# Attention with the values as the stationary operand, a position-major bias table, and ScalarE taking over the rounding and the head outputs

## The reference

```
s_win = einsum(q, k_band) + bias        # window of 8 x 16 positions, relative position bias
s_win = where(col_ok, s_win, NEG_INF)
s_ctx = einsum(q, k_ctx)
p = softmax(concat([s_win, s_ctx]))
o = p_win @ v_band + p_ctx @ v_ctx      # 8 heads of 64 columns
y = real(fft2(f))                       # Fourier branch, 4 groups of 128 channels
mix = (sigmoid(ga) * (y @ w_fourier) + sigmoid(gb) * (o @ w_na_out)) @ w_out
```

## Time and profile before

| | |
|---|---|
| median of 3 runs | 2649.9 us (2649.89 to 2650.17) |
| the profiled execution | 2653.5 us |
| its span | 2651.7 us |
| PE busy | 2619.6 us, 99% |
| PE weight loads busy | 2589.6 us, 98% |
| DVE busy | 2066.4 us, 78% |
| ACT busy | 1059.4 us, 40% |
| mean DMA rate | 111 GB/s |

### The profile page before, as it was taken

The page is one execution under the profiler, slowest core; times in us unless marked ns, Lnnn a source line. Parts: engine busy times, 40 slices in busy tenths (PEclk is TensorE's granted clock), DMA queues, the critical chain, the costliest instruction groups (busy, mean ns, idle before and its releaser), DMA issues.

```text
span 2651.7 us, 46222 instructions
## 1 busy us (share of the span) xinstructions
PE 2619.6 (99%) x18014; PEld 2589.6 (98%) x18014; DVE 2066.4 (78%) x3929; ACT 1059.4 (40%) x1866; POOL 0.2 (0%) x4
## 2 busy tenths in 40 slices
PE   8999999999999999999999999999999999999998
PEld 8999999999999999999999999999999999999997
DVE  7787986867766888798688888777786568987877
ACT  5145253533222534525352534534332225253453
POOL 0000000000000000000000000000000000000000
PEclk9999999999999999999999999999999999999998
DMA  7433422312333132242223242222313322324321
GB/s 281 138 111 106 166 93 98 120 69 98 112 127 124 67 112 96 93 161 95 96 96 120 87 150 104 95 106 98 114 65 127 137 69 101 115 87 151 113 100 58
DMA packets 77804, 295.38 MB, mean 111 GB/s; under 512 B 25168, under 2 KB 31568, under 8 KB 54096
## 3 DMA queue, kind: packets, MB, share of 16 engines
q1 hardware_dynamic: 51552, 211.16, 22.4%
q10 hardware_dynamic: 26096, 82.16, 8.8%
HBM read 289.62 MB, written 6.82 MB: 112 GB/s over the span
## 4 chain that ended last, share of the span: by engine, by line
PE 93%; DVE 4%; DMA 1%; issue 1%; ACT 1%; SPq 0%; ACTq 0%; DVEq 0%
PE psum L799 10%; PE psum L804 10%; PE psum L803 10%; PE psum L539 5%; PE psum L542 5%; PE psum L541 5%; PE psum L588 4%; PE psum L587 4%; PE psum L584 4%; PE psum L1102 3%; PE psum L1105 3%; PE psum L1104 3%; PE psum L688 2%; PE psum L693 2%; PE psum L692 2%; PE psum L900 2%
## 5 line engine op out<-in xcount | busy, mean ns | idle before, releaser
L804 PE MATMUL psum<-Th,w_lo 128*128 128x320 f32 x1024 | 316.4, 309 | 0.0
L799 PE MATMUL psum<-Th,w_hi 128*128 128x320 f32 x1024 | 316.3, 309 | 0.0
L803 PE MATMUL psum<-Tl,w_hi 128*128 128x320 f32 x1024 | 316.1, 309 | 0.0
L1163 ACT ACTIVATE w_hi<-w_raw 128x2048 fp32r<-128x2048 f32 x96 | 183.5, 1911 | 273.4 <-DVE acc L1728 119.8
L539 PE MATMUL psum<-Hh,w_hi 128*128 128x320 f32 x896 | 277.2, 309 | 3.3 <-DVE Hl L2032 2.4
L542 PE MATMUL psum<-Hh,w_lo 128*128 128x320 f32 x896 | 276.7, 309 | 0.0
L541 PE MATMUL psum<-Hl,w_hi 128*128 128x320 f32 x896 | 276.6, 309 | 0.0
L1645 DVE TENSOR_TENSOR w_lo<-w_raw,w_hi 128x2048 fp32r<-128x2048 f32 x96 | 219.6, 2288 | 54.5 <-ACT w_hi L1163 53.5
L799 PE MATMUL psum<-Uh,w_hi 128*128 128x320 f32 x768 | 237.5, 309 | 0.0
L803 PE MATMUL psum<-Ul,w_hi 128*128 128x320 f32 x768 | 237.2, 309 | 0.0
L804 PE MATMUL psum<-Uh,w_lo 128*128 128x320 f32 x768 | 236.6, 308 | 0.0
(11 more groups left out here) (348 smaller groups left out, 7243.8 us busy)
## 6 DMA issues: line engine op xcount, KB each, us to landing
w_raw<-in_wstream SPq DMA_DIRECT2D x184, 1024.0 KB, 4.8
ada_w<-in_ada ACTq DMA_DIRECT2D x145, 512.0 KB, 3.4
first_w<-in_ada SPq DMA_DIRECT2D x9, 512.0 KB, 14.8
first_w<-in_ada_first SPq DMA_DIRECT2D x6, 512.0 KB, 8.8
gath<-in_rpb SPq DMA_DIRECT2D x128, 24.0 KB, 3.5
G<-gath ACTq DMA_DIRECT2D x4, 768.0 KB, 4.7
X<-in_xT SPq DMA_DIRECT2D x8, 320.0 KB, 15.3
yT<-X SPq DMA_DIRECT2D x8, 192.0 KB, 1.9
```

What stands on the lines that cost most here:

```text
L799: m1 = pe.matmul(out, hi[:, k, :], rh, start=(start and k == 0), stop=False, skip_group_check=not start)
L803: pe.matmul(out, hi[:, k, :], rl, start=False, stop=False, skip_group_check=not start)
L804: mm = pe.matmul(out, lo[:, k, :], rh, start=False, stop=(k == 3), skip_group_check=not start)
L1163: act.activation(hi, w_raw[:, r, :, :], ACT.Copy).then_inc(s_whi, 1)
```

## The change

1. The values become the stationary operand, the turned probabilities move. The outputs of the two heads of a step go to the partitions 0 to 63 and 64 to 127 of one PSUM bank, tile by tile in turn. The output is then already turned: `Otok` becomes `OT`, the 20 transposes go, and one pair of VectorE instructions splits all of it.
2. The scale by the reciprocal sum can't be applied to such an output (it would differ by column), so VectorE scales the probabilities in place, before they are turned, at the start of step n for pair n-1. The transposes wait for that (`probs_scaled`) and no longer for the exponentials.
3. ScalarE stores the head outputs (one 128x128 copy per step) and rounds the Fourier pieces; VectorE keeps the subtraction.
4. The bias table is stored with the grid row innermost, so that L2269's operand is contiguous; it is gathered with 16 DMAs in place of 128. The tables are made at steps 1, 2, 3, 4 and (two) 6, not 1, 2, 3, 5, 6, 7.
5. The second `round_tile` of a stage moves on ScalarE from step 6 to step 5, and the second `low_tile` on VectorE from step 7 to step 5.

More of the change, by code:

```diff
@@ L469, in _ @@
         def _(pe):
-            C = make("tile use full h u mean sum sqsum var att sc max exp pt ptc o of fill fev mix mrg opsplit prod snap tlow".split(), u=0)
+            C = make("tile use full h u mean sum sqsum var att sc max scl pt ptc o of fill fev mix mrg opsplit prod snap tlow".split(), u=0)
             tile, use = C["tile"], C["use"]
@@ L890, in attention @@
                     if n >= 2:
[L891 to L903, removed]
+                        pe.wait_ge(s_ptc, C["ptc"].next(2))
+                        if n == 2:
+                            all_evacuated()
+                        if n >= 4:
+                            pe.wait_ge(s_of, C["of"].next())
+                        j = UNIT[2 * n - 4][1]
[7 more added lines that the diff above has]
+                        mm.then_inc(s_o, 1)
+                        C["o"].next()
                     if 1 <= n <= STEPS:
@@ L1143, in _ @@
         def _(act):
-            C = make("use full func mods u32 u xc sq added var std xn y att max exp pt ptc o mrg ada kv wraw whi wsum prod snap late add hsum tsum".split())
+            C = make("use full func mods u32 u xc sq added var std xn y att max exp pt ptc o of fill fhi mrg ada kv wraw whi wsum prod snap late add hsum tsum".split())
             use = C["use"]
@@ L1499, in ffn, with attention @@
                     last_products(l, s, [spare_f, spare_g], True, LATE_PAIRS)
-            def attention():
-                for n in range(STEPS + 1):
+            def attention(hh):
+                for n in range(STEPS + 2):
+                    if 1 <= n <= PIECES:
+                        round_piece(n - 1)
                     if n < STEPS:
@@ L1623, in _ @@
         def _(dve):
-            C = make("use full func h mods u32 u mean sum sq sqsum added std xc xn att kv max sc exp of fill fev pt o mix mrg ada dve whi ophi opsplit wsum prod snap late add hsum hhi tsum thi tlow".split())
+            C = make("use full func h mods u32 u mean sum sq sqsum added std xc xn att kv max sc exp scl of fhi fill fev pt o mix mrg ada dve whi ophi opsplit wsum prod snap late add hsum hhi tsum thi tlow".split())
             use = C["use"]
@@ L2273, in attention @@
-                    if n >= 2:
[L2274 to L2280, removed]
-                    if n in (2, 7):
+                    if n == 1:
+                        dve.wait_ge(s_att, C["att"].next(64 if hh == 0 else 32))
@@ new lines, in attention @@
+                    if n in BIAS_STEPS:
+                        dve.wait_ge(s_max, C["max"].at())
+                    for step in BIAS_STEPS.get(n, ()):
+                        p, kind = divmod(step, 3)
+                        for h in (2 * p, 2 * p + 1):
+                            g = G[:, h, BIAS_OFF[kind] * ROWS:(BIAS_OFF[kind] + WCOLS) * ROWS]
+                            slot = 2 * (step % 2) + h % 2
+                            dve.tensor_tensor(bm[:, slot, 0:256], mask[:, kind, :], g, ALU.subtract).then_inc(s_dve, 1)
+                            bias_at[step] = C["dve"].next()
@@ L2394, in mixing @@
                     dve.wait_ge(s_kv, C["kv"].next(32))
-                for c in range(4):
-                    u = use_no[0]
-                    dve.wait_ge(s_full, C["full"].next())
-                    split_from(bank(u, 0, 0, LAT), Oh[:, c, 0:LAT], Ol[:, c, 0:LAT])
-                    free(split_from(bank(u, 1, 0, P), Oh[:, c, LAT:T], Ol[:, c, LAT:T]))
+                dve.wait_ge(s_of, C["of"].at())
+                split_from(OT[:, :, :], Oh[:, :, :], Ol[:, :, :])
                 link(dve.tensor_copy(Yh[:, :, :], y32[:, :, :]))
@@ L2524, in window_masks, with bias_rows @@
     return out.reshape(P, 3, WCOLS * ROWS)
+def bias_rows(rpb):
+    wide = np.pad(rpb.reshape(DEPTH * HEADS, 2 * ROWS - 1, 2 * WIN - 1), ((0, 0), (0, 0), (16, 17)))
+    rows = [wide[:, ROWS - 1 - r:2 * ROWS - 1 - r].transpose(0, 2, 1) for r in range(ROWS)]
+    return np.ascontiguousarray(np.stack(rows, axis=1)).reshape(DEPTH * HEADS, ROWS, -1)
 def small_waves():
```

89 lines of the change are left out of this document (39 added, 50 removed).

## The result

| | before | changed |
|---|---|---|
| median | 2650.0 us (2649.9 to 2651.0, 4 runs) | 2633.8 us (2633.2 to 2634.6, 4 runs) |
| profiled execution | 2653.5 | 2633.2 |
| its span | 2651.7 | 2631.4 |
| PE busy | 2619.6 | 2594.3 |
| DVE busy | 2066.4 | 2046.9 |

The ratio is 0.9933, with a 95% interval of 0.9922 to 0.9944: 16.3 us faster between the medians, where 14 were forecast.

The account below looks back on a forecast made before the run. TensorE, busy 99%, bounds the kernel. Stages gain 10.4 us and layer ends 3.6, together 14.0: the profiled 2653.5 becomes 2639.5, and 3.6 less for the median gives 2636 us (chance 0.50), range 2626 to 2649.

Parts of the forecast that it names:

- step 6: Attention stage: TensorE's transposes wait 1.8 us for VectorE's scaling queued behind `low_tile`; the step 1.3 us longer.
- step 3: Attention stage: transposes wait for the first scaling behind VectorE's weight subtraction, a gap of 0.7 us.
- Head outputs: TensorE's 12 instructions of a latent step fall from 1.39 to 0.76 us; context steps from 0.50 to 0.32.
- step 4: Attention stage, a latent step without new waits: the plain gain of the head outputs, 0.63 us.
- not side by side: Rival: the two heads don't run in parallel on TensorE, heads stay at 1.4 us; 2648 us, chance 0.15.
- exposed weight loads: Rival: head outputs' weight loads can't hide beside matmuls, 2.9 us a step in place of 0.76; 2700 us, chance 0.10.
- Step 1: First stage of a layer: scaling ends the transposes 0.8 us late, two times in the program.
- Step 5: Attention stage: piece 5 waits for VectorE's subtraction of piece 4, so the gain is 0.48 us.
- Steps 7 to 11: End of an attention stage, 17.0 us before: shorter heads and no `low_tile` wait in step 8, gain 3.5 us.
- A scaled row: VectorE's `tensor_scalar` of 384 elements: 0.36 us for one, 0.65 for two in a row.
- End of a layer: Last heads to gates: 2.82 us becomes 1.0, gain 1.8, twice: 3.6 us.
- Clock: TensorE's clock falls twice, in the first layer's stages, 1.5 us each; rival of six or more falls 2642 us, chance 0.15.

Follow-up runs that it names:

- run 1: Changed kernel with the three tiles of one head issued before those of the other, not alternating; 2638.5 us.
- run 2: Changed kernel without VectorE's scaling of the probabilities, transposes waiting for the exponentials, head outputs left undivided; 2625.4 us.
- run 3: Changed kernel with the second rounding and subtraction of a weight tile back in steps 6 and 7; 2633.3 us.
- run 6: Changed kernel with VectorE's weight tiles at the ends of steps 3 and 6, not 2 and 5, and one bias table each at 5 and 6; 2626.6 us.
- run 7: Changed kernel with ScalarE's two DMA issues for the context keys and values behind its first exponentials, not ahead; 2632.1 us.
- run 8: Changed kernel with the moves of run 6 and run 7 together; 2625.4 us.

## Why the prediction was right

The measured 2633.8 lies 2.2 us below the forecast of 2636, and the forecast's case was the one that came. That the total is so near is in part luck: of the terms of the last stage, step 6 came 0.45 us shorter than forecast and step 3 0.37, while the gains of the other steps together were 0.4 smaller. TensorE's busy time fell by 25.3 us and the span by 20.3, so the new waits are 5 us more than the old ones. By its steps:

- **Head outputs**: 0.76 us forecast, 0.81 measured (0.108 for each of six pairs and 0.16 once). The six transposes behind them take 0.05 longer than before (0.63 and 0.58), which the forecast left out: a latent step without waits, step 4, is 0.53 us shorter, not 0.63. Context steps: 0.32 forecast, 0.37 measured. The rate taken from the scores in two row halves, 0.055 per instruction, is that of two column halves. The rival "not side by side" has fallen, and so has the one of exposed weight loads: alternating, the loads start with the matmuls, two in 0.108 us. The bound that I gave it, 1.4 us without the pairing, is right for a single head in a row (0.109 each) but not for this order, as run 1 showed with 1.08.
- **Step 6**: a gap of 1.8 us forecast (1.7 by the forecast's own times, 562.5 and 564.2), 1.39 measured, with the cause shown by runs 2, 3 and 6. What was off is in the main ScalarE's time: its head output copy begins before the copy ahead of it has ended and the rounding again, 0.1 us each, so that the rounding began 3.8 us after the scores of its step (558.81 against 555.05), not 4.0.
- **Step 3**: a gap of 0.7 forecast, 0.21 measured in three stages (the transposes began 0.58 us after the context heads began, 0.37 without a wait). The weight tile began 3.0 us after the scores of step 2, not the 3.3 of the forecast: the reciprocals (0.13) stand behind it now, and two tables start 0.33 us apart. In the second layer's first stage the gap is 0.56:

```profile
1833.98 0.44 PE L906 MATMUL psum<-PT,V 128*64 128x128 f32 x4
1834.91 0.88 PE L917 MATMUL psum<-ident,pr 128*128 128x128 f32 x6 [0.49 <-DVE pr L2269]
```

  VectorE began the scores of step 2 0.35 us later there; why, stays open.
- **Step 1**: 0.8 forecast. Against a second stage, TensorE stands 0.87 and 0.54 us longer in the two first stages. Against the kernel before, step 1 is only 0.58 and 0.54 longer, since there too the transposes of the first layer's first stage paused for the second exponential.
- **Step 5**: 0.48 forecast, 0.45 measured. **Steps 7 to 11**: 3.5 and 3.3 in the last stage. The sum of that stage is 3.0 forecast and 3.4 measured; that of the second layer's first stage 2.2 and 2.5.
- **A scaled row**: 0.36 us forecast for 384 elements, 0.417 measured, and 0.75 for two in a row, not 0.65. It was read from a cast; why the scaling takes longer was not tried.
- **End of a layer**: 1.0 us forecast, 1.0 measured: 0.5 for ScalarE's copy, and 0.5 from its end (1947.09) to the first gate matmul. That a transposing stream no longer covers the branch is the likely reading of the second half; it was not tried.
- **Missed**: 0.9 us between the stages. In the second layer, before, two instructions there started 0.85 us apart (1909.60 to 1910.44), of which TensorE stood 0.57 for the values' store on VectorE:

```profile
1910.44 0.39 PE L938 MATMUL psum<-w_hi,Uh 128*128 128x256 f32 x1 [0.57 <-DVE V L2353]
```

  In the changed kernel the distance is 0.26, without a wait. That VectorE comes to that stretch earlier is the likely reason.
- **Clock**: the forecast kept two falls, and none came in a stage of any of the eleven profiled executions, the changed kernel's and the ten runs'. By the earlier trace rows a fall is 1.5 us, and 2.9 of the first layer's extra gain agree. But the medians do not hold all of it. The kernel before spreads over 2649.0 to 2653.7 us; its runs over 2653 us have a mean clock of 0.996 and those under 2650 have 0.998, and the profiled execution that the sum was made against, 2653.5 us at 0.996, was among the longest. So the 3.6 us that I took off for the median were, most likely, in the main these two falls; no trace of the kernel before without a fall is kept to show it. Counted so, the forecast of 2636 had no falls in it on either side, and is to be held against the 15.4 us of the second layer's gain, doubled, and the 0.9 between the stages: 16.3. That this is the measured number to a tenth is chance, since single runs differ by more.
- **A rival's sum**: for weight loads that come out from behind, 2.94 less 0.76 us over 32 steps is 70 us and not 68, so 2706 and not 2700. Nothing hangs on it.

Where the gain of the new heads went: 32 latent steps x 0.58 us are 18.6, of which 1.6 go to the transposes behind them, and the end of a layer gives 3.6. Behind the scaling 8.2 came back as waits, which runs 6, 7 and 8 got back by moving what stood ahead of it.

## What to carry to other kernels

When an operation is moved ahead of what the bounding engine waits for, look at what already stands in that queue in the step before: here two weight subtractions of 2.3 us a stage, one of which itself waited for a rounding in the same step, made the scaling cost TensorE 6.8 us in steps 3 and 6, where run 8 shows that it need cost nothing. Move the filler work behind the awaited one and give it a whole step between its own producer and itself. And for small outputs, two matmuls into different partition halves of a bank bring their whole gain only when they alternate (0.81 us a step, 1.08 with one head after the other, 1.39 before): the pairing brings it, not the exchange of the operands.

## What was not expected of the hardware

- Two fp32 matmuls of 128 columns in two column halves of the array take 0.108 us together, the same as one, and start 0.007 us apart. Their weight loads (0.137 us long, against 0.19 for those of the head outputs before) also run two at a time while matmuls in the same rows run. So the rule of the Trainium skill ("TensorE: Matmul & The Clock Gate", Part 3, The mechanism), that loads overlap with running matmuls only in other row groups, does not hold for column halves in this trace. The same section also lets a load into the background weight buffer go ahead of running matmuls, and that would fit the trace.
- Instructions of the two halves overlap even when they don't alternate, where one head's row ends and the other's begins: 0.053 us apart over six instructions in run 1.
- The kernel before seems to run with and without its two falls of the clock: runs of it differ by 4.7 us, with mean clocks of 0.996 to 0.998. In run 3 TensorE stood idle for 0.59, 0.52 and 0.73 us at nearly the same place and the clock did not fall.
